# A two-block transformer kernel on one core: two tiles on the unnormalised input at three norms, and the first mixer's attention work gathered at fewer places

## The reference, cut to what matters

```python
def rms_norm(x, gain):
    y = xf * lax.rsqrt(jnp.mean(xf * xf, axis=-1, keepdims=True) + RMS_EPS)
    return (y * gain.astype(jnp.float32)).astype(x.dtype)

for i in range(DEPTH):                       # first block
    hn = rms_norm(h, attn_norm[i])
    mix = dilated_attention_mixer(hn, ...) if i % 2 == 0 else gla_mixer(hn, ...)
    h = h + mix
    h = h + swiglu(rms_norm(h, ffn_norm[i]), ffn_w_gate_up[i], ffn_w_down[i])

def modulate(h, shift, scale):               # second block, six norms with a shift
    return h * (1 + scale[:, None, :]) + shift[:, None, :]
```

## Time and profile before

| | |
|---|---|
| median of 3 runs | 3609.67 us |
| profiled execution | 3606.76 us |
| its span | 3605.0 us |
| PE busy | 3559.6 us (99%) |
| DVE busy | 2027.0 us (56%) |
| ACT busy | 1295.0 us (36%) |
| mean time of L1704 (`w_lo`) | 1199 ns |
| mean time of L1821 (`xT` plus an evicted tile) | 691 ns |
| mean time of L1877 (conditioning product) | 1813 ns |
| DMA | 107 GB/s over the span |

### The profile page before, as it was taken

The page is one execution under the profiler, slowest core; times in us unless marked ns, Lnnn a source line. Parts: engine busy times, 40 slices in busy tenths (PEclk is TensorE's granted clock), DMA queues, the critical chain, the costliest instruction groups (busy, mean ns, idle before and its releaser), DMA issues.

```text
span 3605.0 us, 46520 instructions
## 1 busy us (share of the span) xinstructions
PE 3559.6 (99%) x17492; PEld 2868.3 (80%) x17492; DVE 2027.0 (56%) x3405; ACT 1295.0 (36%) x2112; POOL 63.8 (2%) x122
## 2 busy tenths in 40 slices
PE   8999999999999999999999999999999999999999
PEld 7777777888866788888888877888888887778887
DVE  5777776655766565656333667433453347574334
ACT  4445544322343232233222444323332334433222
POOL 0000000000000000000000000000000000000000
PEclk9999999999999999999999999999999999999999
DMA  4222223555511255652323222223223322223332
GB/s 142 74 74 74 73 66 106 195 175 193 195 65 53 70 191 178 221 190 95 96 92 100 77 75 76 92 94 99 93 93 94 99 90 83 67 71 99 98 95 82
DMA packets 142009, 387.14 MB, mean 107 GB/s; under 512 B 21648, under 2 KB 62992, under 8 KB 141840
## 3 DMA queue, kind: packets, MB, share of 16 engines
q1 hardware_dynamic: 126928, 306.39, 26.8%
q0 software_dynamic: 14912, 78.52, 6.4%
HBM read 381.85 MB, written 2.10 MB: 107 GB/s over the span
## 4 chain that ended last, share of the span: by engine, by line
PE 89%; DVE 6%; issue 3%; ACT 2%; DMA 0%; SPq 0%; DVEq 0%; ACTq 0%
PE psP L1087 25%; PE psP L1092 24%; PE psP L1088 24%; PE psP L1242 3%; PE psP L1249 3%; PE psP L1243 3%; PE psS L1305 1%; PE psS L1588 1%; PE psM L1611 1%; PE psS L1179 1%; PE psS L1471 1%; PE psS L1455 0%; DVE w_lo L1704 0%; DVE w_more_lo L1934 0%; DVE w_lo L1934 0%
## 5 line engine op out<-in xcount | busy, mean ns | idle before, releaser
L1087 PE MATMUL psP<-h_hi,w_hi 128*128 128x512 f32 x2664 | 1054.0, 396 | 6.3 <-ACT h_hi L700 3.5
L1088 PE MATMUL psP<-h_hi,w_lo 128*128 128x512 f32 x2664 | 1038.8, 390 | 0.0
L1092 PE MATMUL psP<-h_lo,w_hi 128*128 128x512 f32 x2664 | 1029.1, 391 | 0.0
L1704 DVE TENSOR_TENSOR w_lo<-raw,w_hi 128x1024 fp32r<-128x1024 f32 (+1 forms) x465 | 557.6, 1199 | 412.2 <-ACT w_hi L657 405.2
L663 ACT ACTIVATE ybuf<-psP 128x512 f32<-128x512 f32 (+1 forms) x401 | 239.4, 597 | 1232.8 <-PE psP L1092 1231.3
L1087 PEld LDWEIGHTS psP<-h_hi,w_hi 128*128 128x128 f32 x2664 | 500.6, 188 | 134.0 <-issue 33.2
L1092 PEld LDWEIGHTS psP<-h_lo,w_hi 128*128 128x128 f32 x2664 | 498.6, 188 | 108.5 <-DVE h_lo L1785 5.0
L1088 PEld LDWEIGHTS psP<-h_hi,w_lo 128*128 128x128 f32 x2664 | 501.1, 188 | 98.9
L657 ACT ACTIVATE w_hi<-raw 128x1024 fp32r<-128x1024 f32 (+1 forms) x465 | 480.7, 1034 | 102.7 <-PE psP L1092 102.7
L1087 PE MATMUL psP<-a_hi,w_hi 128*128 128x512 f32 x1248 | 492.7, 395 | 1.2 <-ACT a_hi L1040 1.2
L1088 PE MATMUL psP<-a_hi,w_lo 128*128 128x512 f32 x1248 | 486.0, 389 | 0.0
(11 more groups left out here) (320 smaller groups left out, 3565.1 us busy)
## 6 DMA issues: line engine op xcount, KB each, us to landing
raw<-in_gu SPq DMA_DIRECT2D x264, 512.0 KB, 3.4
adaw<-in_ada POOLq DMA_DIRECT2D x96, 768.0 KB, 5.1
raw<-in_down SPq DMA_DIRECT2D x96, 448.0 KB, 3.3
raw<-in_down SPq DMA_DIRECT2D x48, 512.0 KB, 3.5
raw<-in_qkv SPq DMA_DIRECT2D x40, 512.0 KB, 3.9
raw<-in_mix_in SPq DMA_DIRECT2D x34, 512.0 KB, 3.3
raw<-in_qkv SPq DMA_DIRECT2D x64, 256.0 KB, 3.0
raw<-in_wo SPq DMA_DIRECT2D x32, 512.0 KB, 3.3
```

What stands on the lines that cost most here:

```text
L1087: nc.tensor.matmul(psP[:, s, :], hi, rhs[0](kt), start=(n == 0), stop=False)
L1088: nc.tensor.matmul(psP[:, s, :], lo, rhs[0](kt), start=False, stop=False)
L1092: mm = nc.tensor.matmul(psP[:, s, :], w_hi[:, s, kt * P:kt * P + P], rhs[1](kt), start=False, stop=(n == K - 1))
L1704: v.tensor_tensor(w_lo[:, s, 0:cols], raw[:, s, 0:cols], w_hi[:, s, 0:cols].bitcast(F32), ALU.subtract)\
```

## The change

**Three norms.** While the stage before ends, ACT and DVE split `xT` times gain, piece by piece, without the factor (`raw_high`, `raw_low`, one piece behind `residual`): into `a_hi`/`a_lo` for `N_ffn0`, into `h_hi`/`h_lo` for the other two. PE's `norm` is gone at these three places, with its `keep_warm` matmuls. `two_ahead` takes the next stage's first two tiles in lockstep on that unnormalised input, with the two `token_sums` behind steps 0 and 2 and `spread` behind step 4. ACT copies the spread factor from PSUM into SBUF (`row`, which is the buffer `acc`), and the eight pieces are normalised as before, for the third tile on. In the two stages that hold the unnormalised input in `h_hi`/`h_lo`, a normalised piece waits until both tiles have used the old one (`raw_used`). The third tile waits per step for its piece. The first two tiles are multiplied by `row` at their eviction: in the FFNs by DVE from PSUM (`scaled_by_row`), with ACT's Silu on the result; in GLA by DVE from `ybuf`, where it used to copy.

**Conditioning product.** In the third part of the two FFNs none of it stands behind the down tiles any more; the pairs have 16 instead of 12, and its sums on PE stand in the fourth down tile instead of the last.

**Attention places.** `weigh` and `turn_qk` move to the place of `scores` (step 3), `turn_qk` in the other tiles to that of the first `turn`. ACT does `head_rstd` ahead of `mixed` and `turned_qk`, and the first `copied` ahead of the weight split.

```diff
-ADA_PAIRS = {8: (2, 1, 2, 1, 2, 1, 2, 1), 7: (2, 2, 1, 2, 2, 2, 1)}
-ADA_DOWN = 4
+ADA_PAIRS = ((2, 1, 2, 1, 2, 1, 2, 1), (2, 2, 1, 2, 2, 2, 1), (3, 2, 2, 2, 3, 2, 2))
+ADA_DOWN = (4, 4, 0)
...
+            def raw_high(N, m, last=False):
+                if last:
+                    act.wait_ge(evac_done, pos.count(RING))
+                else:
+                    act.wait_ge(y_used, pos.count(RING))
+                nc.scalar.activation(raw_split(N)[0](m), xT[:, m, :], copy, scale=gain_of(N, m)).then_inc(raw_hi, 1)
...
+                if warm_up:
+                    nc.scalar.activation(warm[:, :], ident[:, 0:1], warm_up)
+                if N in AHEAD:
+                    act.wait_ge(N.bc_ready, N.turns(l) + 1)
+                    nc.scalar.activation(row[:, :], psS[:, 0, 0:T], copy).then_inc(r_ready, 1)
...
+            def first_pair(N):
+                act.wait_ge(pair_scaled, AHEAD[N] // 2 + 1)
+                s = pos.slot()
+                nc.scalar.activation(ybuf[:, s, :], ybuf[:, s, :], ACT.Silu).then_inc(evac_done, 1)
+                pos.step()
+                hi(2, D)
+                pos.step()
+                hi(2, D)
+                act.wait_ge(evac_done, pos.count(RING))
...
+            def two_ahead(N):
+                rhs = raw_split(N)
+                slot_ready(0)
+                slot_ready(1)
+                for kt in range(KT):
+                    pe.wait_ge(raw_hi, KT * AHEAD[N] + kt + 1)
+                    for a in range(2):
+                        highs(rhs, kt, kt, pos.slot(a))
+                    pe.wait_ge(raw_lo, KT * AHEAD[N] + kt + 1)
+                    lows(KT, rhs, kt, kt, pos.slot(0))
+                    mm = lows(KT, rhs, kt, kt, pos.slot(1))
+                    if kt < KT - 1 and N is not N_ffn0:
+                        mm.then_inc(raw_used, 1)
+                    if kt == 0:
+                        pe.wait_ge(N.head_ready, N.turns(0))
+                        token_sums(acc, psM).then_inc(N.head_stat, 1)
+                    elif kt == 2:
+                        pe.wait_ge(N.acc_ready, N.turns(0) + 1)
+                        token_sums(sq, psS[:, 1, T:2 * T]).then_inc(N.stat_ready, 1)
+                    elif kt == 4:
+                        spread(N, 0, psS[:, 0, 0:T])
...
-                    if n == 0:
+                    if n == 0 and F.norm in AHEAD:
+                        two_ahead(F.norm)
+                        tile(KT, h_split, before=lambda kt: pe.wait_ge(F.norm.h_ready, F.norm.turns(l) * KT + kt + 1))
+                        tiles(2 * nf - 3, KT, h_split)
...
+                g, odd = divmod(m - 15, 2)
+                if g >= 0 and not odd:
+                    if g:
+                        at_step(3, weigh, g - 1)
+                    at_step(3, scores, g)
                 if m >= 10:
-                    at_step(2, turn_qk, m - 2)
+                    at_step(3, turn_qk, m - 2)
...
-            norm(N_ffn0, 0)
             ffn(F0, 0)
-            norm(N_gla, 0)
...
+            def raw_low(N, m):
+                dve.wait_ge(raw_hi, KT * AHEAD[N] + m + 1)
+                hi, low = raw_split(N)[0](m).bitcast(F32), raw_split(N)[1](m)
+                v.scalar_tensor_tensor(low, xT[:, m, :], gain_of(N, m), hi, ALU.mult, ALU.subtract).then_inc(raw_lo, 1)
...
+            def scaled_by_row(of_pair):
+                dve.wait_ge(tile_done, pos.count(RING + 1))
+                dve.wait_ge(y_used, pos.free(0))
+                if of_pair:
+                    dve.wait_ge(evac_done, pos.count(RING))
+                s = pos.slot()
+                return v.tensor_tensor(ybuf[:, s, :], psP[:, s, :], row[:, :], ALU.mult)
...
                 g = ybuf[:, pos.slot(), :]
+                if raw:
+                    scaled_by_row(False).then_inc(pair_scaled, 1)
                 pos.step()
                 lo_of(2, ahead[0])
+                if raw:
+                    scaled_by_row(True).then_inc(evac_done, 1)
...
-                    used(v.tensor_copy({"z": zg, "q": qg, "k": kg}[kind][:, :], y(32 if kind == "z" else P)))
+                    rows = 32 if kind == "z" else P
+                    dst, yk = {"z": zg, "q": qg, "k": kg}[kind][:, :], y(rows)
+                    used(v.tensor_tensor(dst, yk, row[0:rows, :], ALU.mult) if i < 2 else v.tensor_copy(dst, yk))
```

More of the change, by code:

```diff
@@ L711, in ffn @@
                         after_second()
-                    with tile_loop(act, pos, nf // 3, 6):
+                    pairs = nf
+                    if n == 0 and N:
+                        first_pair(N)
+                        pairs -= 1
+                    with tile_loop(act, pos, pairs // 3, 6):
                         for j in range(6):
@@ L845, in _ @@
                     turned_qk(m - 2)
-                if k >= 8:
-                    head_rstd(k)
+                g, odd = divmod(m - 15, 2)
+                if g >= 0 and odd:
+                    copied(2 * g)
                 for n in weight_tiles_of(m):
@@ L870, in _ @@
             mixed(7)
-            project()
-            norm(N_ffn0, 0, h_split[0])
-            ffn(0, (D, D, D))
+            project(None, N_ffn0)
+            norm(N_ffn0, 0, h_split[0], warm_up=ACT.Silu)
+            ffn(0, (D, D, D), N=N_ffn0, ahead=N_gla)
             norm(N_gla, 0, h_split[0])
@@ L941, in _ @@
             hi(2, D)
-            project()
-            norm(N_ffn1, 0, h_split[0])
-            ffn(0, (D, D, D), after_second=rotation)
+            project(None, N_ffn1)
+            norm(N_ffn1, 0, h_split[0], warm_up=ACT.Silu)
+            ffn(0, (D, D, D), after_second=rotation, N=N_ffn1)
             for l in range(2):
@@ L1518, in _ @@
                     at_step(5, turn_out, GLA_TILES[i][1])
-                tile(KT, h_split, beside=steps)
+                tile(KT, h_split, beside=steps,
+                     before=(lambda kt: pe.wait_ge(N_gla.h_ready, N_gla.turns(0) * KT + kt + 1)) if i == 2 else None)
             two_tiles(KT, a_split, lambda kt, low: pe.wait_ge(gmix_ready, kt + 2))
             tiles(KT - 2, KT, a_split)
-            norm(N_ffn1, 0)
             ffn(F1, 0)
@@ L1894, in ffn @@
                     for j in range(rest):
-                        gated(a_at(nf - rest + j), F, l * FT + (f0 + nf - rest + j), shapes[2 * j + 3:2 * j + 5])
-                        for _ in range(ADA_PAIRS[nf][j]) if g is not None else ():
+                        gated(a_at(nf - rest + j), F, l * FT + (f0 + nf - rest + j), shapes[2 * j + 3:2 * j + 5],
+                              n == 0 and j == 0 and F.norm in AHEAD)
+                        for _ in range(ADA_PAIRS[n][j]) if g is not None else ():
                             ada(c_ada)
```

76 lines of the change are left out of this document (56 added, 20 removed).

## The result

The changed kernel takes 3630.68 us (median of 5 runs, 3627.31 to 3631.37) against 3609.67 us (3604.68 to 3610.88): the ratio is 1.0060, 95% interval 1.0045 to 1.0074. It is 21 us slower. The prediction was 3612 us, with a range to 3626 us; the measured time lies outside it.

A forecast was written before the change was run, and what follows sets the result against it. PE, busy 99% of the span, was taken to bound the kernel. Norms +7.05, clock +3.7 and attention -7.0 gave +3.75 us on the 3609.67 us median: 3613, rounded to 3612 us, range 3596 to 3626 us.

The forecast's parts named there:

- The adapter products moved into the pairs: FFN pairs: DVE would be busy 9.7 of 10.9 us at worst with the moved products; costed at 0.
- The norms: The three changed norms, without any change of clock: 0.8 + 4.35 + 1.9 = 7.05 us slower.
- Fourth tile at ffn1: Norm at ffn1: fourth tile waits for its weight split, starting at 24.65 instead of 22.78, 1.9 us lost.
- v tile: Gated mixer (GLA): the chain behind normalisations, weight splits, scaled tiles and logits comes 4.35 us later.
- the clock: PE's granted clock falls at all three norms: 1.5 us at each FFN norm, 0.7 at the mixer, 3.7 in sum.
- The split of the unnormalised input: Last projection's tiles before the norms: extra ACT and DVE operations, hidden by PE; uncovered, up to 0.75 us a tile.
- The rival in which each norm gains 4.2 us: Norms hidden as the two tiles suggest, each boundary keeping 4.2 us: 20.6 faster, 3589 us; chance 0.15.
- Attention: Attention places, joined sites and shorter waits together: 7.0 us won, bounds 2 and 11.
- the joining: Attention on PE: three sites per two tiles joined, saving 0.11 us a pair, 3.2 us over 29 pairs.
- The waits' gain: Attention: half of PE's 7.3 us of waits for probabilities and their copies goes, taken as 3.8 us.
- the scores now stand ahead of the transposed queries, so that chain is 0.23 us earlier: Attention on PE: scores' new place makes their chain 0.23 us earlier, a reason for the 3.8 us of waits won.
- The rival of 3621 us: Stall at third and fourth tile rules, slow clock at all three norms, attention under 4 us: 11 slower; chance 0.25.

The follow-up runs named there:

- either half: Kernel before with PE's attention places alone: 3606.11 us, ratio 0.9995; kernel before with ACT's attention order alone: 3605.53 us, ratio 0.9993.

## Why the prediction was wrong

- **The step that failed** is "The adapter products moved into the pairs: 9.7 of 10.9 us on DVE at worst. I cost it at 0." The pairs are indeed free. But the same edit moves the second half's sums on PE from the last down tile to the fourth, and that move is in no term of the sum. It adds a wait on PE with a slow stretch behind it, 20.2 us by itself. The trace of before had the price: DVE's `mods` (L1864 there), which the moved sums need, came at 978.11, and ACT began to evict the third down tile at 974.17. PE reaches the sums one step of 0.68 us into the fourth tile, so 3.4 us of waiting could be read off (978.11 + 0.16 - 974.17 - 0.68; it became 3.64), and the half clock behind a pause of PE stood in the earlier trace rows. The text before the prediction names the move, but no step asks who still holds those twelve columns.

```profile
978.11 0.16 DVE L1864 TENSOR_TENSOR mods<-psS,par 128x12 f32<-128x12 f32 x1
```

- **The norms** were right in mechanism and nearly in size. Fourth tile at ffn1 +2.2 (1.9 forecast), at ffn0 +1.0 (630.64 - 605.79 = 24.85 against 23.83; forecast 0.8), v tile +4.9 (4.35): 8.1 us against 7.05. The run with the norms alone is 13.1 slower, which leaves 5.0 for the clock and what else lies behind, against 3.7. Of it 1.7 us are the clock behind each FFN norm's wait (0.83 over 10 us at ffn0, 0.76 over 7 us at ffn1, with the norms alone). GLA's 2.8 us at half clock lie within its 4.9, in place of the wait that was to grow by 1.5. The other 1.6 isn't pinned down; GLA's later pauses vary by as much. The split of the unnormalised input is hidden. The rival in which each norm gains 4.2 us is out.
- **Attention** brought 14.6 instead of 7.0 (12.9 in its stretch), beyond its bound of 11. The term that was mis-sized is the joining: 0.28 us a pair instead of 0.11, 7.8 us instead of 3.2, since the seam between weighted sums and scores was allowed 0.05 and is worth 0.20. The waits' gain was 5.1 instead of 3.8. That the copy ahead of the weight split helps was right. That "the scores now stand ahead of the transposed queries, so that chain is 0.23 us earlier" left out that ACT's `head_rstd` was tied to those queries.
- **The sum** would have been 13.1 - 14.6 = -1.5 without the missed term, and the kernel after with the sums put back measures 3609.88, no change. The forecast of 3612 was near that by luck, through two errors of opposite sign in its known terms (2.4 too little for the norms, 7.6 too little for attention). The rival of 3621 us gave the right side for another reason: its condition, under 4 us from attention, didn't come true. Two of the prediction's sums are slightly off and change nothing here: the terms of the mixer's third tile end at 26.7 and not 26.9, and 3609.67 + 3.75 is 3613.4, not 3612.

The best kernel of all these is the attention change alone, 3594.20 us.

## What to carry to other kernels

When work is moved on one engine, list what each moved instruction waits for, also for the release of a buffer that it overwrites, and look up in the trace of before when that releaser runs; a move of a few 1-column matmuls can cost more than a redone norm. Price a new pause of TensorE with the slow stretch behind it, which here cost about twice the pause at the sums (6.4 and 7.7 us behind 3.64) and less than the pause at the norms. And when sites are joined on the engine that bounds, re-order the engines that feed it in the same step: here either half looked nearly worthless alone.
